# A doubling inverse without identity products, and sums of squares added one tile late

## What is computed

```python
def wkv7_scan(r, decay, k, v, a, b):
    # per head, state S (v_dim x k_dim):
    # S_t = S_{t-1} diag(decay_t) + (S_{t-1} a_t) b_t^T + v_t k_t^T ;  y_t = S_t r_t
    ...
x = x + 0.5 * swiglu(rms_norm(x, ffn_norm[l, 0]), ffn_w_in[l, 0], ffn_w_out[l, 0])
h = rms_norm(x, mix_norm[l])
x = x + rwkv7_time_mix(h, ...)
```

## Time and profile before

| | us |
|---|---|
| median of 3 runs (3501.64 to 3502.81) | 3502.67 |
| the profiled execution | 3507.43 |
| its span | 3505.6 |
| TensorE busy | 3188.5 (91%) |
| VectorE busy | 1696.9 (48%) |
| ScalarE busy | 1161.2 (33%) |
| GpSimd busy | 142.9 (4%) |
| mean granted TensorE clock | 0.911 of full speed |

### The profile page before, as it was taken

The page is one execution under the profiler, slowest core; times in us unless marked ns, Lnnn a source line. Parts: engine busy times, 40 slices in busy tenths (PEclk is TensorE's granted clock), DMA queues, the critical chain, the costliest instruction groups (busy, mean ns, idle before and its releaser), DMA issues.

```text
span 3505.6 us, 38393 instructions
## 1 busy us (share of the span) xinstructions
PE 3188.5 (91%) x15360; PEld 2547.2 (73%) x15360; DVE 1696.9 (48%) x2759; ACT 1161.2 (33%) x1871; POOL 142.9 (4%) x145
## 2 busy tenths in 40 slices
PE   7999798888888889999999997779999879988997
PEld 6888476677777778887788885458888356877886
DVE  5434543455555554344743447755434345336235
ACT  3323133434443343233332233543223233323332
POOL 0000000112111100000000000000000000000000
PEclk9999898778776899999999998689999979997998
DMA  3333231000000033332233322013333410201231
GB/s 126 98 97 96 64 102 34 3 3 3 4 3 13 1 121 101 97 97 95 79 96 102 93 82 75 1 30 97 97 98 95 154 51 1 76 19 46 79 96 54
DMA packets 173895, 234.75 MB, mean 67 GB/s; under 512 B 14201, under 2 KB 111062, under 8 KB 173462
## 3 DMA queue, kind: packets, MB, share of 16 engines
q1 hardware_dynamic: 173718, 232.29, 21.5%
HBM read 228.05 MB, written 4.19 MB: 66 GB/s over the span
## 4 chain that ended last, share of the span: by engine, by line
PE 82%; DVE 10%; ACT 4%; issue 2%; DMA 1%; POOL 0%; SPq 0%; DVEq 0%; ACTq 0%
PE banks L796 60%; PE banks L1221 3%; PE banks L889 2%; PE banks L1215 1%; PE banks L927 1%; PE banks L951 1%; PE banks L1209 1%; PE banks L957 1%; PE banks L1161 1%; PE banks L955 1%; PE banks L901 1%; DVE diff_scores L2177 1%; DVE diff_small L2183 1%; PE banks L860 1%; PE banks L948 1%
## 5 line engine op out<-in xcount | busy, mean ns | idle before, releaser
L1756 DVE TENSOR_TENSOR weights_lo<-weights_raw,weights_hi 128x1024 fp32r<-128x1024 f32 (+2 forms) x393 | 473.1, 1207 | 1034.4 <-ACT weights_hi L1289 1033.2
L796 PE MATMUL banks<-operand_hi,weights_hi 128*128 128x512 f32 x2208 | 874.2, 396 | 35.6 <-DVE weights_lo L1756 20.9
L796 PE MATMUL banks<-operand_lo,weights_hi 128*128 128x512 f32 x2208 | 867.3, 393 | 0.0
L796 PE MATMUL banks<-operand_hi,weights_lo 128*128 128x512 f32 x2208 | 867.1, 393 | 0.0
L1289 ACT ACTIVATE weights_hi<-weights_raw 128x1024 fp32r<-128x1024 f32 (+2 forms) x393 | 407.9, 1041 | 1096.4 <-PE banks L796 1040.4
L796 PEld LDWEIGHTS banks<-operand_hi,weights_hi 128*128 128x128 f32 x2208 | 419.3, 190 | 130.9 <-issue 25.5
L796 PEld LDWEIGHTS banks<-operand_lo,weights_hi 128*128 128x128 f32 x2208 | 419.4, 190 | 89.5 <-issue 2.4
L796 PEld LDWEIGHTS banks<-operand_hi,weights_lo 128*128 128x128 f32 x2208 | 419.1, 190 | 88.8
L796 PE MATMUL banks<-hidden_ffn_hi,weights_hi 128*128 128x512 f32 x352 | 136.9, 389 | 0.0
L796 PE MATMUL banks<-hidden_ffn_lo,weights_hi 128*128 128x512 f32 x352 | 136.9, 389 | 0.0
L796 PE MATMUL banks<-hidden_ffn_mid_hi,weights_hi 128*128 128x512 f32 x352 | 136.9, 389 | 0.0
(11 more groups left out here) (517 smaller groups left out, 4700.8 us busy)
## 6 DMA issues: line engine op xcount, KB each, us to landing
weights_raw<-in_ffn_w_in_dram SPq DMA_DIRECT2D x352, 256.0 KB, 3.1
weights_raw<-in_ffn_w_out_dram SPq DMA_DIRECT2D x88, 512.0 KB, 3.7
weights_raw<-in_w_in_dram SPq DMA_DIRECT2D x36, 512.0 KB, 3.6
weights_raw<-in_rwkv_w_rkv_dram SPq DMA_DIRECT2D x24, 512.0 KB, 3.9
weights_raw<-in_w_mod_dram SPq DMA_DIRECT2D x24, 512.0 KB, 4.6
weights_raw<-in_w_kv_dram SPq DMA_DIRECT2D x16, 512.0 KB, 3.6
weights_raw<-in_rwkv_w_o_dram SPq DMA_DIRECT2D x8, 512.0 KB, 5.2
weights_raw<-in_diff_w_q_dram SPq DMA_DIRECT2D x8, 512.0 KB, 4.6
```

The source lines that it names most:

```text
L796: mm = nc.tensor.matmul(o, l, r, start=first and t == 0 and job["opens"], stop=last and t == 2, **skip)
L1756: nc.vector.tensor_tensor(ring_lo[0:p, u["slot"], 0:n, 0:w], ring_raw[0:p, u["ring"], 0:n, 0:w], f32(ring_hi[0:p, u["slot"], 0:n, 0:w]), A ...
```

## The change

The unit diagonal of I - M is put into the tile itself. `ar` loses its sign (L1964, event `ma`), so `mq` holds -M; POOL adds the identity to the half that is inverted (event `mi`), after DVE's second mask and before its two other operations; ACT's `mh` and DVE's `ml` come after it. POOL's mask of `inv_t` now also brings the diagonal, so that it makes `mi`, `inv` and `invt`, three operations as before. The level masks have the unit diagonal and the sign, so `xm` is I plus the old `xm`, and the products of step d need no identity product: 4 matmuls for each bank, 8 in `refine`, 4 in `full`. `2I - x` is made when the bank of `refine` is read, by DVE (event `rx`) in place of ACT. DVE's and ACT's copies of `nv` and of the turned `a` carry the sign. In front of the stage one operation of DVE writes 2I where there were five.

The sums of squares are taken one tile behind: DVE adds tile k to x, then the square of tile k - 1 (with `put_lo` of k - 1 where `fed` holds it), and the last one after the loop.

```diff
-            act += ["rx", "full", "w", "var", "std", "yl"]
-            dve += ["nv", "bonus0", "bonus", "gh0", "gh1", "z"]
+            act += ["full", "w", "var", "std", "yl"]
+            dve += ["rx", "nv", "bonus0", "bonus", "gh0", "gh1", "z"]
...
-            pool = ["b2", "k3", "inv", "seed", "invt", "g", "clear"] + (["sb0"] if half else [])
+            pool = ["b2", "k3", "mi", "inv", "invt", "g", "clear"] + (["sb0"] if half else [])
...
-        ident4, neg_ident = op[1][:, 2], op[1][:, 3, 0:P]
-        identr = ident4[:, 0:P]
+        two_ident = op[1][:, 2, 0:P]
...
-                    nc.tensor.matmul(ps[:, b], identr, joined(L.inv_t), start=True, stop=False, skip_group_check=True)
                     pe.wait_ge(*by_dve.at(at(f"xm{lv}")))
                     for p in range(4):
-                        mm = nc.tensor.matmul(ps[:, b, p * P:(p + 1) * P], L.xm[:, p], L.inv_t[:, p], start=False,
-                                              stop=True, skip_group_check=True)
+                        mm = nc.tensor.matmul(ps[:, b, p * P:(p + 1) * P], L.xm[:, p], L.inv_t[:, p], start=True, stop=True)
                     mm.then_inc(*by_pe.by(at(f"t{lv}")))
                     b = bank(f"i{lv}")
-                    nc.tensor.matmul(ps[:, b], identr, joined(L.inv), start=True, stop=False, skip_group_check=True)
                     for p in range(4):
-                        mm = nc.tensor.matmul(ps[:, b, p * P:(p + 1) * P], L.inv_t[:, p], L.xm[:, p], start=False,
-                                              stop=True, skip_group_check=True)
+                        mm = nc.tensor.matmul(ps[:, b, p * P:(p + 1) * P], L.inv_t[:, p], L.xm[:, p], start=True, stop=True)
                     mm.then_inc(*by_pe.by(at(f"i{lv}")))
                 elif step == "refine":
                     b = bank("rx")
-                    nc.tensor.matmul(ps[:, b], identr, ident4, start=True, stop=False, skip_group_check=True)
                     pe.wait_ge(*by_act.at(at("ii4")))
-                    nc.tensor.matmul(ps[:, b], neg_ident, joined(L.inv), start=False, stop=False, skip_group_check=True)
                     pe.wait_ge(*by_dve.at(at("ml")))
                     for p in range(4):
                         for part in (L.mh, L.ml):
-                            mm = nc.tensor.matmul(ps[:, b, p * P:(p + 1) * P], part[:, p], L.inv[:, p], start=False,
-                                                  stop=True, skip_group_check=True)
+                            mm = nc.tensor.matmul(ps[:, b, p * P:(p + 1) * P], part[:, p], L.inv[:, p],
+                                                  start=part is L.mh, stop=part is L.ml)
                     mm.then_inc(*by_pe.by(at("rx")))
...
                 elif step == "full":
                     b = bank("full")
                     pe.wait_ge(*by_act.at(at("it4")))
-                    nc.tensor.matmul(ps[:, b], identr, joined(L.inv_t), start=True, stop=False, skip_group_check=True)
-                    pe.wait_ge(*by_act.at(at("rx")))
+                    pe.wait_ge(*by_dve.at(at("rx")))
                     for p in range(4):
-                        mm = nc.tensor.matmul(ps[:, b, p * P:(p + 1) * P], L.xm[:, p], L.inv_t[:, p], start=False,
-                                              stop=True, skip_group_check=True)
+                        mm = nc.tensor.matmul(ps[:, b, p * P:(p + 1) * P], L.xm[:, p], L.inv_t[:, p], start=True, stop=True)
...
-                    act.wait_ge(*by_dve.at(at("mq1")))
+                    act.wait_ge(*by_pool.at(at("mi")))
                     nc.scalar.activation(L.mh, L.mq[:, :, 0, :], ACT.Copy).then_inc(*by_act.by(at("mh")))
...
-                elif step == "refine":
-                    act.wait_ge(*by_pe.at(at("rx")))
-                    nc.scalar.activation(L.xm, blocks(ps[:, bank("rx")]), ACT.Copy).then_inc(*by_act.by(at("rx")))
...
-                            if part:
-                                fed(k)
+                            if part and k:
+                                fed(k - 1)
+                    if part:
+                        fed(KC - 1)
...
-            for j in range(4):
-                nc.vector.tensor_copy(ident4[:, j * P:(j + 1) * P], ident[:, :])
-            nc.vector.tensor_scalar(neg_ident, ident[:, :], -1.0, None, ALU.mult).then_inc(*wkv_ready.by(0))
+            nc.vector.tensor_scalar(two_ident, ident[:, :], 2.0, None, ALU.mult).then_inc(*wkv_ready.by(0))
...
-                    nc.vector.scalar_tensor_tensor(out=L.ar[:, :, 0, :], in0=blocks(L.t[5]), scalar=-1.0,
-                                                   in1=blocks(L.t[6]), op0=ALU.mult,
-                                                   op1=ALU.mult).then_inc(*by_dve.by(at("ma")))
+                    nc.vector.tensor_tensor(L.ar[:, :, 0, :], blocks(L.t[5]), blocks(L.t[6]),
+                                            ALU.mult).then_inc(*by_dve.by(at("ma")))
...
                 elif step == "refine":
+                    dve.wait_ge(*by_pe.at(at("rx")))
+                    nc.vector.scalar_tensor_tensor(out=L.xm, in0=blocks(ps[:, bank("rx")]), scalar=-1.0,
+                                                   in1=f32(two_ident).unsqueeze(1).broadcast_to([P, 4, P]), op0=ALU.mult,
+                                                   op1=ALU.add).then_inc(*by_dve.by(at("rx")))
                     dve.wait_ge(*by_pe.at(at("nv")))
-                    nc.vector.tensor_copy(L.av[:, :, HEAD:P], ps[:, bank("nv"), 0:HT].rearrange(
-                        "p (q v) -> p q v", q=4)).then_inc(*by_dve.by(at("nv")))
+                    nc.vector.tensor_scalar(L.av[:, :, HEAD:P], ps[:, bank("nv"), 0:HT].rearrange("p (q v) -> p q v", q=4),
+                                            -1.0, None, ALU.mult).then_inc(*by_dve.by(at("nv")))
...
-                                add_square(stage, k, free)
+                                if k:
+                                    add_square(stage, k - 1, free)
+                            if bi:
+                                add_square(stage, KC - 1, free)
...
-                    add_square("w_out", k, rms_sum.at("cq"))
+                    if k:
+                        add_square("w_out", k - 1, rms_sum.at("cq"))
+            add_square("w_out", KC - 1, rms_sum.at("cq"))
...
-            i4 = f32(ident4).rearrange("p (b t) -> p b t", t=P)
+            i4 = ident[:, :].unsqueeze(1).broadcast_to([P, 4, P])
...
+                    pool.wait_ge(*by_dve.at(at("mq1")))
+                    nc.gpsimd.tensor_tensor(L.mq[:, :, 0, :], L.mq[:, :, 0, :], i4, ALU.add).then_inc(*by_pool.by(at("mi")))
                     pool.wait_ge(*by_dve.at(at("sd1")))
                     nc.gpsimd.tensor_tensor(L.inv, f32(L.inv), i4, ALU.add).then_inc(*by_pool.by(at("inv")))
+                    pool.wait_ge(*by_pool.at(at("mi")))
                     nc.gpsimd.tensor_tensor(L.inv_t, L.mq[:, :, 0, :], seed[:, 1].unsqueeze(1).broadcast_to([P, 4, P]),
-                                            ALU.mult).then_inc(*by_pool.by(at("seed")))
-                    pool.wait_ge(*by_pool.at(at("seed")))
-                    nc.gpsimd.tensor_tensor(L.inv_t, f32(L.inv_t), i4, ALU.add).then_inc(*by_pool.by(at("invt")))
+                                            ALU.mult).then_inc(*by_pool.by(at("invt")))
                 elif step == "full":
                     pool.wait_ge(*by_dve.at(at("nv")))
...
-    t["seed"] = f(np.concatenate([near & (i > j), near & (i < j)], 1))
-    t["level"] = f(np.concatenate([(i // (2 * s) == j // (2 * s)) & (i % (2 * s) >= s) & (j % (2 * s) < s)
+    unit = (i == j).astype(np.int32)
+    t["seed"] = f(np.concatenate([0 - (near & (i > j)), unit - (near & (i < j))], 1))
+    t["level"] = f(np.concatenate([unit - ((i // (2 * s) == j // (2 * s)) & (i % (2 * s) >= s) & (j % (2 * s) < s))
                                    for s in (2, 4, 8, 16, 32)], 1))
     t["run"] = f(np.broadcast_to(np.arange(T // 2) % CHUNK != 0, (P, T // 2)))
```

More of the change, by code:

```diff
@@ L352, in wkv_uses @@
                 use += [(f"t{lv}", "act", f"it{lv}"), (f"i{lv}", "act", f"ii{lv}")]
-            use += [("rx", "act", "rx"), ("nv", "dve", "nv"), ("full", "act", "full"), ("w", "act", "w"),
+            use += [("rx", "dve", "rx"), ("nv", "dve", "nv"), ("full", "act", "full"), ("w", "act", "w"),
                     ("bon", "dve", "bonus"), ("gh0", "dve", "gh0"), ("gh1", "dve", "gh1"), ("z", "dve", "z")]
@@ L1452, in act_program @@
                     if lv == 1:
-                        nc.scalar.activation(L.av[:, 0:2, 0:HEAD], blocks(ps[:, b, 0:HT])[:, :, 0:HEAD], ACT.Copy)
-                        nc.scalar.activation(L.av[:, 2:4, 0:HEAD], blocks(ps[:, b, 0:HT])[:, :, HEAD:P],
-                                             ACT.Copy).then_inc(*by_act.by(at("tr1")))
+                        nc.scalar.activation(L.av[:, 0:2, 0:HEAD], blocks(ps[:, b, 0:HT])[:, :, 0:HEAD], ACT.Copy,
+                                             scale=-1.0)
```

(2 more changed lines are left out.)

## The result

The changed kernel takes 3528.0 us in the median of 19 runs (3502.0 to 3541.0), the kernel before 3508.9 on the same occasions (3485.9 to 3523.5). The ratio is 1.0048, with a 95% interval of 1.0025 to 1.0071: about 17 us slower, where 38.5 us faster was forecast.

What follows compares the result with a forecast made beforehand. A TensorE-bound scan stage with waits as holes: -63 products, +15 waits, +4 GpSimd, -0.6 copies, -3.9 sums, +10 clock = -38.5 us, so 3468.9 profiled, 3464 median; range 3438 to 3493.

Steps and rivals of the forecast that it cites:

- the clock's term: Scan stage: granted clock falls two points, 0.76 to 0.74, at 5 us each, costing 10 us.
- The sign that the forecast had named against itself: Scan stage: forecast is wrong if the granted clock moves by more than four points.
- The third rival: Scan stage: without full-width identity products clock falls 12 points, costing 60 us; 3514 us, slower; break-even 10 points; chance 0.05.
- the no-change case: Scan stage: clock just above the break-even of about 0.66, so no change in time; chance 0.07.
- The price of a point: Scan stage: a hundredth of granted clock costs 3.6 to 7.4 us; 5 taken.
- The path's terms: Scan stage: 63 us of identity products go, 15 return as waits, GpSimd's addition and new waits cost 4.
- the last rival: Step d: first product behind a wait pays the start L948 paid, at most 12 us; 3476 us; chance 0.10.
- the lower bound: Path to step x: GpSimd's inv takes 1.27 us after mi, so is ready 0.1 us later.
- the 20 that I had named as proof against me: Scan stage: forecast is wrong if TensorE's waits for xm and inv grow by more than 20 us.
- Sums of squares: Taken one tile behind: 1.9 us gained at the first layer, 2.0 at w_out, 3.9 together.
- a third place that I had put at nothing: Second and third layer and after rwkv_o: sum over channels follows TensorE's own products, so nothing gained.
- a rival with five points: Scan stage turns to latencies: longer waits, clock five points (25 us) lower; worst corner -6.5 us, middle 3483 us; chance 0.20.

Runs made afterwards that it cites:

- e6: Changed kernel plus 80 meaningless 512-column products behind the wait for xm, between step d's two groups of four; 3541.2 us, ratio 1.0094.
- e10: Changed kernel plus 112 meaningless 512-column products: 80 ahead of the waits for xm, the others ahead of those of refine and full; 3538.1 us, ratio 1.0088.
- e4: Changed kernel plus 80 meaningless 512-column products, one per step d ahead of the wait for xm; 3486.9 us, ratio 0.9942 against the kernel before.
- e12: Changed kernel plus 80 meaningless 512-column products at the head of step x, behind the wait for the evacuated inverse; 3523.2 us, ratio 1.0040.
- e1: Kernel before with only the sums of squares taken one tile behind, old inverse kept; 3499.0 us, ratio 0.9969.

## Why the prediction was wrong

**The step that failed is the clock's term.** The forecast had two points at 5 us each, 10 us; no row stood behind the two. The scan shows eight points (0.756 to 0.677) at 7 us each, 57 us, in a profile that is one of the faster runs. The sign that the forecast had named against itself, more than four points, came. The third rival had the course right (without the products the clock falls, and takes more than they gave) and named 12 points, 60 us; its reason, full-width work as such, does not order the runs (e6 and e10 against e4); its break-even, put at ten points, lay nearer seven at the true price. That rival and the no-change case beside it together had a chance of 0.12, and "against" it stood the sentence that slow products fill the holes themselves. They do: waits fill 12% of the time at 1.2 GHz in both kernels. But that did not keep the fast stretches long. What shrank is the fast stretch, from 15.6 to 8.9 us in the mean, and there the waits take 28% in place of 19%. The error was to reason on the mean busy share of the stage, which hardly moves (slots are 84% of the scan before and 82% after), when the earlier trace rows show two regimes, of which only the fast one has more waits now.

That the clock and not something else pays rests on three things: the work stays within 2% in kernels with the same products, while the clock moves from 0.744 to 0.797 or from 0.647 to 0.677; e4 takes 41 us off the changed kernel with products that compute nothing; and within the 19 runs of the changed kernel the time follows the clock of the run (0.899 with 3502.0 us, 0.883 to 0.886 with 3539.6 to 3541.0; correlation -0.97). What tips the clock in one place and not in another was not shown (e6, e10 and e12 against e4).

The Trainium skill (TensorE: Matmul & The Clock Gate, HAM oscillation — how this bites in real kernels) says that waits between bursts send the array back to half speed, and advises keeping it fed. The direction was right: the kernel with more waiting at full speed has the lower clock. As a recipe it isn't enough here: e10 waits less than e4 (105.9 against 110.9 us) and has the lower clock, 0.678 against 0.711 in the scan and 0.894 against 0.907 over all runs.

**The price of a point** lay inside its bounds of 3.6 and 7.4 us, but at the upper end: all of TensorE's slots scale with the clock, those in front of waits too. 366 us of work divided by the clock: 366/0.746 - 366/0.756 is 6.5 us for a point at the high end, 366/0.677 - 366/0.687 is 7.9 at the low one.

**The path's terms were right in sum.** Predicted -63 for the products, +15 for waits behind them, +4 for GpSimd: -44. Measured -58 of work and +16 of waits: -42. The split differs, and the sum is right by luck: in the measured terms the forecast took 83 us of slots away and let the waits grow by 39 (the 20 of slots that lay under a wait, 15 and 4), so both were off by some 25 us, which cancels. All 208 products at 0.28 us would be 58 us at 2.4 GHz, and only 44 went, so 14 us at that clock stay with the products that are left. That is the size of the last rival (at most 12 us for a start that moves to the first product behind a wait); nothing here shows whether it is that.

**GpSimd and the new waits.** Step `pairs` of the item at 873 us after the change (start us, us, engine, line, what [idle before <-releaser]):

```profile
873.01 1.29 DVE L1920 TENSOR_TENSOR m_q<-banks,masks 128x512 f32<-128x512 f32 x2 [2.04 <-PE banks L888]
...
874.38 1.27 POOL L2433 TENSOR_TENSOR m_q<-m_q,ident 128x512 f32<-128x512 f32 x1 [3.13 <-DVE m_q L1920]
...
875.60 1.27 POOL L2435 TENSOR_TENSOR operand_hi<-operand_hi,ident 128x512 fp32r<-128x512 f32 x1
875.68 0.63 ACT L1438 ACTIVATE operand_hi<-m_q 128x512 fp32r<-128x512 f32 x1 [3.59 <-POOL m_q L2433]
...
876.35 1.08 DVE L1971 TENSOR_TENSOR operand_lo<-m_q,operand_hi 128x512 fp32r<-128x512 f32 x1 [1.38 <-ACT operand_hi L1438]
876.83 1.72 POOL L2437 TENSOR_TENSOR operand_hi<-m_q,seed_masks 128x512 fp32r<-128x512 f32 x1
877.02 0.87 PE L926 MATMUL banks<-operand_hi 128*128 128x128 f32 x4 [1.97 <-POOL operand_hi L2435]
```

`mi` takes 1.27 us, `inv` after it 1.27 (1.26 to 1.28 in all 16 items), in place of 1.77 in the earlier trace rows: the lower bound, as taken. The cost fell on VectorE: `ml` 1.08 us in place of 0.69, a little below the 1.3 expected. And GpSimd's `invt`, with VectorE beside it, got the 1.72. The Trainium skill (SBUF — State Buffer, Who interferes with whom) has one port pair that the two engines lock for an instruction at a time, who issues first going first; these rows agree: `ml`, begun while `inv` ran, takes 1.08 us, and `invt`, begun while `ml` ran, 1.72. TensorE's waits for `inv` grew by 3.1 us and those for `xm` by 8.1: 11.2 together, below the 20 that I had named as proof against me.

**Sums of squares** came as forecast at the two places. At the end of the first layer, the chain of the changed kernel in order of time (start us, us, what):

```profile
387.78 0.70 DVE x_turned L1819
388.48 0.02 issue
388.50 0.64 ACT squares L1294
389.14 0.03 issue
389.17 0.70 DVE squares_sum L1763
389.88 0.04 issue
389.92 1.14 PE banks L808 x2
```

Before, L808's counterpart started at 391.73; TensorE's last product ended at the same time, so 1.8 us are gained where 1.9 was expected. At `w_out` TensorE stands 2.2 us between its last product and the sum over channels, in place of 4.3: 2.1, expected 2.0. There was a third place that I had put at nothing. At the end of the second layer's last block the kernel before has this in its chain:

```profile
2113.12 4.23 DMA weights_raw<-in_diff_w_q_dram
2117.35 0.02 issue
2117.38 1.06 ACT weights_hi L1289
2118.44 0.02 issue
2118.47 1.24 DVE weights_lo L1756
2119.70 0.04 issue
2119.74 5.26 PE banks L796 x15
```

The sums held back the next weights' load, and TensorE stood for 2.1 us at 2119.7. In e1 the chain there is TensorE alone:

```profile
2104.82 20.20 PE banks L796 x88
```

Its longest wait for VectorE's low part of the weights is still the one at the start of `rwkv_o` (9.1 us). So 6 us for the sums in place of 3.9; e1 measured 0.3%, some 11 us, with an interval of 4 to 18.

**The range** was too narrow on the slow side, and for the same reason: its upper end came from a rival with five points, while the earlier trace rows contain no bound for the clock at all. Even the worst corner of that rival, 3496 us, lay outside the 3493 of the range. The mean over two levels that alternate in stretches of 9 to 16 us came out anywhere from 0.64 to 0.80 in the 20 kernels here, and a range that rests on it should say so.

## What to carry over

Where TensorE's clock sits between its two levels in a stage, work taken out of that stage can be paid back by the clock: divide the work by the clock (here 410/0.756, then 366/0.677) and give the clock's term bounds as wide as the stage is mixed. Try the same edit in another weave of the lanes before judging it; one constant made the kernel before 0.5% faster and did not help the changed one (1.0065 and 1.0048, with intervals that overlap). Redundant full-width products ahead of a wait can be worth their place, but measure each place, for more of them isn't better.

## What the runs showed that I had not expected

- Eighty products of 512 columns that compute nothing made the changed kernel 1.1% faster ahead of a wait, and the same number behind it made it slower still (3486.9 and 3541.2 us, against 3528.0).
- One core alone, with nothing else changed, spreads by 1.1% from run to run (3502.0 to 3541.0), and that goes with its mean granted clock (0.899 to 0.883): about 27 us for a hundredth of the whole run's clock. One profiled execution says little on a difference of half a per cent.
- A GpSimd addition or masking of 128x512 in SBUF takes 1.27 us, or 1.72 to 1.77 in the rows where VectorE began to subtract two SBUF tiles just before it; VectorE's subtraction of that size 0.69 or 1.08.
